# Eight split weight tiles instead of six, and another order of conversions and operand pieces

## The reference

```python
cond = silu(c)
for i in range(2):
    mod = (cond @ ada_w[i] + ada_b[i])[:, None, :]
    shift1, scale1, gate1, shift2, scale2, gate2 = jnp.split(mod, 6, axis=-1)
    h = rmsnorm(x, norm1_g[i]) * (1.0 + scale1) + shift1
    y = diff_attention(h, ...) if i == 0 else axial_gqa(h, ...)
    x = x + gate1 * y
    h = rmsnorm(x, norm2_g[i]) * (1.0 + scale2) + shift2
    x = x + gate2 * swiglu(h, f_w_in[i], f_w_out[i])
x = rmsnorm(x, final_g)

# second block
h = rms_norm(x, mix_norm_g)
z_a, q, k, v, gate_logits = jnp.split(h @ w_in, splits, axis=-1)
y_a = chunked_spatial_gating(gelu(z_a), gmlp_norm_g, w_spatial, b_spatial)
y_b = dilated_mixture_attention(rope(q), rope(k), v)
gates = sigmoid(gate_logits)
x = x + (gates[0] * (y_a @ w_branch_a) + gates[1] * (y_b @ w_branch_b)) @ w_out
up = rms_norm(x, ffn_norm_g) @ w_up
a, val = up[..., :2816], up[..., 2816:]
x = x + (gelu(causal_depthwise_conv(a, conv_w, conv_b)) * val) @ w_down
return rms_norm(x, final_norm_g)
```

## Time and profile before

| | us |
|---|---|
| median of 3 runs | 1038.45 |
| lowest and highest run | 1038.05, 1038.98 |
| the profiled execution: its span | 1033.8 |
| TensorE busy (95%) | 986.3 |
| VectorE busy (72%) | 740.2 |
| ScalarE busy (52%) | 542.6 |
| GpSimd busy (7%) | 68.4 |

### The profile page before, as it was taken

One profiled execution on the slowest core, in us unless ns is written; L12 is line 12 of the kernel. 1 busy time (PEld: TensorE's weight loads), 2 busy tenths in 40 slices (PEclk: granted clock), 3 DMA queues, 4 the chain that ended last, 5 costly groups with the idle time before them and its releaser, 6 DMA issues.

```text
span 1033.8 us, 13550 instructions
## 1 busy us (share of the span) xinstructions
PE 986.3 (95%) x5102; PEld 827.2 (80%) x5102; DVE 740.2 (72%) x1053; ACT 542.6 (52%) x875; POOL 68.4 (7%) x126
## 2 busy tenths in 40 slices
PE   2999799999999999999999999999999999999997
PEld 2887577888878787778888886888888779999986
DVE  5988888878877897887665447647753777777643
ACT  4466846544443485575444436575546474444442
POOL 2100222000000411010000002000000010000000
PEclk8999999999999999999999999999999999999999
DMA  9998167998889472449865553856444367656551
GB/s 339 371 371 285 39 204 230 344 321 295 273 304 359 162 250 101 143 127 321 263 203 186 183 184 108 269 160 205 134 142 143 119 190 218 187 177 189 184 184 41
DMA packets 126968, 219.89 MB, mean 213 GB/s; under 512 B 9235, under 2 KB 78088, under 8 KB 126904
## 3 DMA queue, kind: packets, MB, share of 16 engines
q1 hardware_dynamic: 125200, 215.52, 63.4%
q0 software_dynamic: 1088, 2.87, 0.8%
q10 hardware_dynamic: 616, 0.65, 0.2%
HBM read 217.96 MB, written 1.05 MB: 212 GB/s over the span
## 4 chain that ended last, share of the span: by engine, by line
PE 84%; DVE 8%; ACT 4%; issue 2%; DMA 1%; POOL 0%; SPq 0%; POOLq 0%; DVEq 0%; ACTq 0%
PE bank L1900 13%; PE bank L1902 13%; PE bank L1901 13%; PE bank L1913 5%; PE bank L1915 5%; PE bank L1914 5%; PE bank L2504 3%; PE bank L2505 3%; PE bank L2506 3%; DVE w_lo L1156 2%; PE bank L1961 2%; PE bank L1963 2%; PE bank L1962 2%; ACT w_hi L638 1%; DVE ada_acc L1186 1%
## 5 line engine op out<-in xcount | busy, mean ns | idle before, releaser
L1156 DVE TENSOR_TENSOR w_lo<-raw,w_hi 128x1024 fp32r<-128x1024 f32 x312 | 379.1, 1223 | 215.3 <-ACT w_hi L638 214.5
L638 ACT ACTIVATE w_hi<-raw 128x1024 fp32r<-128x1024 f32 x312 | 328.2, 1061 | 338.4 <-PE bank L1902 139.7
L1900 PE MATMUL bank<-w_hi,h_hi 128*128 128x512 f32 x608 | 244.3, 402 | 3.7 <-DVE w_lo L1156 3.7
L1902 PE MATMUL bank<-w_hi,h_lo 128*128 128x512 f32 x608 | 238.3, 392 | 0.0
L1901 PE MATMUL bank<-w_lo,h_hi 128*128 128x512 f32 x608 | 237.9, 391 | 0.0
L1900 PEld LDWEIGHTS bank<-w_hi,h_hi 128*128 128x128 f32 x608 | 114.8, 189 | 28.4 <-issue 6.1
L1902 PEld LDWEIGHTS bank<-w_hi,h_lo 128*128 128x128 f32 x608 | 114.7, 189 | 24.6
L1901 PEld LDWEIGHTS bank<-w_lo,h_hi 128*128 128x128 f32 x608 | 114.9, 189 | 23.6 <-issue 1.0
L2504 PE MATMUL bank<-h_hi,w_hi 128*128 128x256 f32 x320 | 90.8, 284 | 1.1 <-DVE conv_t L1828 1.1
L2505 PE MATMUL bank<-h_hi,w_lo 128*128 128x256 f32 x320 | 90.7, 283 | 0.0
L2506 PE MATMUL bank<-h_lo,w_hi 128*128 128x256 f32 x320 | 90.7, 283 | 0.0
(11 more groups left out here) (328 smaller groups left out, 1372.2 us busy)
## 6 DMA issues: line engine op xcount, KB each, us to landing
raw<-in_f_w_in SPq DMA_DIRECT2D x176, 256.0 KB
ada<-in_ada_w SPq DMA_DIRECT2D x86, 512.0 KB, 5.9
raw<-in_w_in SPq DMA_DIRECT2D x46, 512.0 KB
raw<-in_f_w_out SPq DMA_DIRECT2D x44, 512.0 KB
raw<-in_w_up SPq DMA_DIRECT2D x88, 256.0 KB
raw<-in_a_w_qkv SPq DMA_DIRECT2D x24, 512.0 KB
raw<-in_w_down SPq DMA_DIRECT2D x22, 512.0 KB
raw<-in_b_w_qkv SPq DMA_DIRECT2D x12, 512.0 KB
```

The lines of the kernel that those rows point to most:

```text
L638: nc.scalar.activation(w_hi[:, m % SPL], raw[:, m % RAW], ACT.Copy).then_inc(hi_done, 1)
L1156: ve.tensor_tensor(w_lo[:, m % SPL], raw[:, m % RAW], w_hi[:, m % SPL].bitcast(F32), ALU.subtract).then_inc(lo_done, 1)
L1900: mm(o, hi, w_hi[:, s, k], start=(u == 0 and k == 0), stop=False)
L1902: last = mm(o, lo, w_hi[:, s, k], start=False, stop=(u == 3 and k == 1))
```

## The change

`SPL` goes from 6 to 8: `w_hi` and `w_lo` have eight slots each, and ScalarE and VectorE run eight tiles ahead. Room for it comes from the places of `w_sp` and `w_spT`, which now lie in two slots of `ada` (the tiles of `ada_w`). Those are free only after fold 95, so GpSimd loads and masks `w_sp` later, before the root of the boundary to the second block; TensorE turns it at tile 12 of `IN_C`, and ScalarE copies the result behind the split at place 15. The side inputs at the start are seven instead of eight. In `boundary`, operand pieces stand ahead of splits and conversions, and on VectorE piece 1 ahead of the residual of the second half. `modulate(1)` comes before `low(7)` and `low(8)` instead of behind `low(6)` alone. `gains_2` converts tiles `WO_A + 10` and `WO_A + 11`. In `feed_forward` and at the start of `w_up`, two splits and conversions instead of four stand before the first chunk is taken, the other two behind it. The entry of `TAKE_AFTER` for vector 9 moves from tile 99 to 101, and the scratch memory for descriptors made on the chip is set to 1024.

```diff
 EPS = 1e-6
-SIDE = 8
+SIDE = 7
 VECS = 11
...
 RAW = 4
-SPL = 6
+SPL = 8
+SCRATCH = 1024
 LOOP = 8
...
 VECTORS = 12
+ADA_END = 96
+SP_TURN, SP_TAKE = 12, 15
...
 REDUCE_AFTER = {59: 6, 72: 7, 93: 9}
-TAKE_AFTER = {68: 6, 81: 7, 99: 9}
+TAKE_AFTER = {68: 6, 81: 7, 101: 9}
...
         rope_c_sb = sb("rope_c_sb", [P, T, 2, 16])
-        w_spT = sb("w_spT", [P, 4, P])
         REG_U = 2 * KF * S * 4
...
         lam_v = at_p("lam_v", [P, 4, 64], 11136)
-        w_sp = at_p("w_sp", [P, 4, P], 9216)
+        w_sp, w_spT = (ada[:, 0, a].rearrange("p (g s) -> p g s", g=4) for a in range(2))
         freq_row = at_p("freq_row", [P, 8], 11392)
...
         setup_t = sem("setup_t")
-        setup_p = sem("setup_p")
+        sp_in, sp_low, sp_t, sp_ok = sem("sp_in"), sem("sp_low"), sem("sp_t"), sem("sp_ok")
         dve = sem("dve")
...
                 slot_free(m, turn)
+                m = at(m, turn, LOOP)
                 src = w.rearrange("(k p) n -> p k n", p=P)[:, 2 * u:2 * u + 2, cols(c0, turn, per, n)]
...
                 slot_free(m, turn)
+                m = at(m, turn, LOOP)
                 v = w.rearrange("(k p) n -> p k n", p=P)
...
             norm(0)
-            pool.wait_ge(ada_done, 8)
-            pool.dma_start(w_sp[:], w_spatial[0].rearrange("g t s -> t g s")).then_inc(side_in, 16)
             lanes = same_lane[:].rearrange("p a n -> p (a n)")
...
                                         pattern=[[-1, P]], channel_multiplier=1).then_inc(lane_ok, 1)
-
-            pool.wait_ge(side_in, 16)
-
-            nc.gpsimd.affine_select(out=w_sp[:], in_=w_sp[:], compare_op=ALU.is_ge, fill=0.0, base=0,
-                                    pattern=[[0, 4], [-1, P]], channel_multiplier=1).then_inc(setup_p, 1)
             pool.wait_ge(ada_done, 12)
...
             pool.dma_start(row[:], final_g.partition_broadcast(P)).then_inc(late_in[1], 16)
+            pool.wait_ge(ada_done, ADA_END)
+            pool.dma_start(w_sp, w_spatial[0].rearrange("g t s -> t g s")).then_inc(sp_in, 16)
+            pool.wait_ge(sp_in, 16)
+            nc.gpsimd.affine_select(out=w_sp, in_=w_sp, compare_op=ALU.is_ge, fill=0.0, base=0,
+                                    pattern=[[0, 4], [-1, P]], channel_multiplier=1).then_inc(sp_low, 1)
             root(3, with_y=True)
...
                 part_operand(o, 0, 1, gain, shift)
+                part_square(r, 1, 0)
+                part_operand(o, 0, 2, gain, shift)
+                part_square(r, 1, 1)
+                part_operand(o, 0, 3, gain, shift)
+                part_scale(r, 1)
                 split(first)
-                part_square(r, 1, 0)
-                part_square(r, 1, 1)
-                part_operand(o, 0, 2, gain, shift)
-                part_operand(o, 0, 3, gain, shift)
-                split(first + 1)
-                part_scale(r, 1)
-                for p in range(2):
+                for p in range(4):
                     part_operand(o, 1, p, gain, shift)
-                split(first + 2)
-                part_operand(o, 1, 2, gain, shift)
-                part_operand(o, 1, 3, gain, shift)
-                split(first + 3)
+                for m in range(first + 1, first + 4):
+                    split(m)
...
                     split(QKV_A + SPL + m)
-                if m == 8:
-                    act.wait_ge(setup_t, 3)
-                    nc.scalar.activation(w_spT[:], bank[7][:].rearrange("p (g t) -> p g t", g=4), ACT.Copy).then_inc(setup, 1)
                 if m == 9:
...
             def feed_forward(base, f, gate_n):
-                for j in range(4):
+                for j in range(2):
                     split(base + SPL + j)
                 silu(base, f, 0, 0)
+                for j in range(2, 4):
+                    split(base + SPL + j)
                 for turn in range(5):
...
                     split(IN_C + SPL + j, turn)
+                    if 8 * turn + j == SP_TAKE:
+                        act.wait_ge(sp_t, 1)
+                        nc.scalar.activation(w_spT, bank[7][:].rearrange("p (g t) -> p g t", g=4), ACT.Copy).then_inc(sp_ok, 1)
                     if j % 4 == 3:
...
             nc.scalar.activation(stat[:, MISC + 7:MISC + 8], stat[:, SS:SS + 1], ACT.Gelu)
-            for j in range(4):
+            for j in range(2):
                 split(UP_C + SPL + j)
             take_first()
+            for j in range(2, 4):
+                split(UP_C + SPL + j)
             for c in range(NCH_FF - 1):
...
                 part_operand(o, 0, 0, gain, shift)
+                part_operand(o, 0, 1, gain, shift)
                 part_residual(r, s, nxt, 1, 1, gated)
-                part_operand(o, 0, 1, gain, shift)
-                low(first)
                 part_operand(o, 0, 2, gain, shift)
                 part_operand(o, 0, 3, gain, shift)
-                low(first + 1)
                 part_scale(r, 1)
...
                     part_operand(o, 1, p, gain, shift)
-                low(first + 2)
+                low(first)
                 part_operand(o, 1, 2, gain, shift)
                 part_operand(o, 1, 3, gain, shift)
-                low(first + 3)
+                for m in range(first + 1, first + 4):
+                    low(m)
...
             low(5)
-            low(SPL)
+            low(6)
             modulate(1)
+            for m in range(7, SPL + 1):
+                low(m)
...
-                v_.wait_ge(setup, 4)
+                v_.wait_ge(setup, 3)
                 link(ve.tensor_tensor(neg_lam, stat[:, MISC + 5:MISC + 6], stat[:, MISC + 4:MISC + 5], ALU.subtract))
...
                 ve.tensor_copy(stat[:, MISC + 7:MISC + 8], stat[:, MISC + 2:MISC + 3]).then_inc(setup_v, 1)
-                v_.wait_ge(setup, 5)
+                v_.wait_ge(setup, 4)
...
                 make_gains(N2_V, 4)
-                low(IN_0)
-                low(IN_0 + 1)
+                low(WO_A + 2 + SPL)
+                low(WO_A + 3 + SPL)
...
             def feed_forward(base, f):
-                for j in range(4):
+                for j in range(2):
                     low(base + SPL + j)
                 glu(f, 0, 0)
+                for j in range(2, 4):
+                    low(base + SPL + j)
                 for turn in range(5):
...
                     reduce_vector(1)
-                if m == 7:
-                    pe.wait_ge(setup_p, 1)
-                    for g in range(4):
-                        last = nc.tensor.transpose(bank[7][:, g * P:(g + 1) * P], w_sp[:, g], ident[:])
-                    last.then_inc(setup_t, 1)
...
                     pe.wait_ge(evac, 9 + m // 4 - 1)
+                if m == SP_TURN:
+                    pe.wait_ge(sp_low, 1)
+                    for g in range(4):
+                        last = nc.tensor.transpose(bank[7][:, g * P:(g + 1) * P], w_sp[:, g], ident[:])
+                    last.then_inc(sp_t, 1)
                 wide(IN_C + m, m % 4, m // 4 % 2, 6)
...
                 pe.wait_ge(gm_v, 1)
+                pe.wait_ge(sp_ok, 1)
                 for t in range(T):
...
-    nc = bacc.Bacc("TRN2", target_bir_lowering=False, num_devices=1)
+    nc = bacc.Bacc("TRN2", target_bir_lowering=False, num_devices=1, dynamic_dma_scratch_size=SCRATCH)
     arrays, args = {}, []
```

## The result

The changed kernel takes 1059.24 us (median of 4 runs, 1058.27 to 1060.3) against 1038.25 us for the kernel before on the same chip: a ratio of 1.0189 with a 95% interval of [1.0171, 1.0208]. It is slower by 21.0 us. The direction is the forecast one, but the size is nearly three times the +7.2 us of the sum and outside the range. Run again beside other kernels it took 1058.35 us, ratio 1.0181 [1.0153, 1.0208].

The account below looks back on a forecast made before the run. TensorE was taken as the bound, busy 986.3 of 1033.8 us. Terms 8.0 + 1.8 + 1.0 - 5.8 + 1.2 + 1.0 = +7.2 us gave span 1041.0, plus 4.65, time 1045.6 us; range 1038.5 to 1050.0.

Parts of the forecast that it names:

- Start, ScalarE: Third operand piece at the start: scaling waits behind two more conversions, 5.0 us later (bounds 4.6 and 5.3).
- Start, VectorE: Rotation of the first queries: two more conversions and two folds ahead; TensorE 8.0 us late, including the ScalarE wait.
- Start of attention: Between second maximum and first `wgt`: two more folds on VectorE, 1.8 us more.
- End of attention: `scale_a(7)` behind four folds instead of two: TensorE stands 1.9 us, 0.9 saved at vector 4's sums, net 1.0 us.
- Boundaries: Between stages and just behind: waits on `h_lo`, `block_sums`, `xn` and the second layer's first activation go, -5.8 us.
- Second layer's attention: A second fold before the last two maxima, +1.2 us.
- w_up: First convolution behind the conversion of tile 12 instead of 10, +1.0 us (bounds 0 and 3.1).
- The first feed-forward: Two tiles more lead while its loads lag: 0 in the sum, 1.2 us kept for the range.
- Rival 1: Faster: data of tiles 8 and 9 land early, the start's loss goes, the waits are gained; 1032.2 us, chance 0.12.
- Rival 4: Nothing: start costs half its term, gains hold, small later terms are 0; +1.0, 1039.5 us, chance 0.13.
- Rival 2: Clock falls after long waits, 1.7 us behind the rotation and again at 144 us; 1047.3 to 1049.0 us, chance 0.25.
- Rival 3: GpSimd's seven small loads at the start are late through the smaller scratch, 7 us more; near 1051 us, chance 0.05.

Follow-up runs that it names:

- f_fill: Changed kernel with the first product six tiles ahead in its old places, the two extra conversions at the end of the first layer's attention; 1054.27 us.
- a_spl6: Changed kernel with six slots instead of eight, two conversions kept ahead of the second half's operand pieces; 1059.43 us, its output not the reference's.
- d_chunks: Changed kernel with every chunk in both feed-forwards and in `w_up` taken two conversions sooner on ScalarE and VectorE; 1044.47 us.
- c_start: Changed kernel with the old places of operand pieces 2 and 3 and of the rotation, at the start alone; 1055.62 us.
- h_warm: Changed kernel with 14 and 12 needless matmuls ahead of the wait on the second `act_u` in each feed-forward; 1058.13 us.
- p_piece: Kernel before with one part alone: on VectorE operand piece 1 ahead of the second half's residual, at all boundaries; 1038.85 us.

## Why the prediction was wrong

By its own steps:

- *Start, ScalarE.* Right in kind. The scaling began at 48.47, 4.5 us late, just under the lower bound of 4.6. Tile 9's load was issued at 42.84, 0.8 us later than before, and its data were there at 47.51, 0.8 us sooner: it took 4.7 us instead of 6.2. I had allowed 0.7 us at most for the missing `w_sp`; whether that load is the whole difference no run shows.
- *Start, VectorE.* 8.0 us forecast, 8.2 measured, of which 1.1 lay ahead of tile 0. In the other profiles tile 0 starts between 1.0 us sooner and 1.7 us later than in that of the kernel before (f_fill, with the old start, has 1.1 too), so this 1.1 is no effect of the change. The change itself cost some 7.1, and that 8.2 fits the 8.0 so well is luck.
- *Start of attention.* 1.8 us forecast, 11.2 - 9.5 = 1.7 measured.
- *End of attention.* 1.0 forecast; the wait on `att` is 1.4 (1.9 forecast) and 0.9 came back at the sums of vector 4, net 0.5.
- *Boundaries.* The waits on `h_lo` and `block_sums` and the one on `xn` ahead of the second layer went as forecast; across the four boundaries the delay falls by 1.6, 2.6, 2.0 and 1.3 us. Behind the last one 0.6 comes back, and in all TensorE's waits on `xn` are 1.4 us in four now (0.6 in one before) and those on `xs` 1.3 (0.8). The 0.8 us at the second layer's first activation did not go: that wait is 1.4 us now.
- *Second layer's attention.* 1.2 forecast, 1.3 measured, and a wait of 1.1 on `proj` (L2228) that I had not looked for.
- *w_up.* +1.0 forecast with an upper end of 3.1; 21.8 - 18.1 = 3.7 measured, of which 2.9 are the wait on `conv_t` (1.1 to 4.0) and 0.7 that on `av` (0.8 to 1.5). I took the nearest TensorE wait where VectorE's own idle row of 3.06 us was the better measure. And the reason given, two more tiles, is not the only one: a_spl6 has the wait without them.
- *The first feed-forward.* This is the step that failed: "The first feed-forward gets two tiles more lead while its loads lag; the nearest row is the 1.2 us wait at L1943, and I put 0 there and keep 1.2 for the range." It cost 3.9 us at the second activation, and the same place in the second feed-forward, which the sum did not name, 3.0 on top of the first activation's 0.6. I had counted lead as something that can only help. The lead is made by conversions, each engine has one row, and I had used precisely that argument at the start and not here. d_chunks prices this step, with `w_up` and the falls of the clock behind the three, at 14.8 us. Without it d_chunks stands at +5.6 us (1044.47 against 1038.85), near the +7.2 of the sum.
- *Rival 1* fell with its condition: tile 9's data were there at 47.51, not before 43.97. *Rival 4* fell too: the start cost 8.2 us, not 4.0.
- *Rival 2.* It named the right mechanism, which came beside the forecast and not instead of it: the clock fell behind the rotation as it said, not at 144 us, and at three places more, since the new long waits were more. That waits as long stand nowhere in the old trace holds only behind its first 26 us, where there are waits of 9.9 and 3.7. The Trainium skill, cited there (TensorE: Matmul & The Clock Gate, section HAM oscillation — how this bites in real kernels), tells this of waits for data of about 3 to 5 us. That was borne out by four falls behind waits of 2.9 to 4.0 us, but not each time: two waits of 3.1 and 3.3 us in other runs (c_start's first `wgt`, h_warm's `w_up`) had none behind them, nor had the 2.6 us wait at tile 6 of the changed kernel.
- *Rival 3* fell: f_fill has the same GpSimd loads and scratch, and its rotation is on time.

The direction was right because the start was read right; the size was wrong because the same reading was not carried through the rest of the program.

## What to carry to other kernels

More buffers between engines let the producer run ahead, but the engine's row decides what pays for it: every step that stands behind the produced tiles in the same row is later by the time that the extra tiles take, or by the wait for their data, and this is worst wherever loads have no lead (the start, behind a boundary). Move such steps ahead by as many tiles as the depth grew; here that turned +2% into -1%. When one place shows this, look for all others of the same form before adding up, and give each new wait on TensorE its price for the clock as well: some 1.5 us, nearly always behind 3 us and more in these traces, and about every second time behind 2 to 3 us.

## What was new about the hardware

The granted clock fell to 0.50 behind single waits in an otherwise busy TensorE: behind 23 of 25 waits of 3.0 to 5.5 us, and behind 16 of 35 waits of 2.0 to 3.0 us. The same wait of 2.49 us on the same instructions had a fall behind it in p_piece and none in the kernel before. Most of these falls lasted 3.4 us, and those of the changed kernel cost 1.3 to 1.6 us each; some lasted 6.8 us, and the one of f_fill from 201.4 us on cost 2.4.
